# Gates, branch outputs and their gated sum computed with tokens on partitions instead of features on partitions

## The reference, cut to what matters

```python
gates = jax.nn.sigmoid((h @ w_gate + b_gate).astype(jnp.float32)).astype(x.dtype)   # 3 x 1024 columns
g_a, g_b, g_c = jnp.split(gates, N_BRANCH, axis=-1)
merged = g_a * (y_a @ w_br_swa) + g_b * (y_b @ w_br_moba) + g_c * (y_c @ w_br_ssd)
x = x + merged @ w_mix_out
```

## Time and profile before

| | |
|---|---|
| median of 3 runs (lowest, highest) | 1179.04 us (1178.24, 1179.38) |
| profiled execution: its time, its span | 1178.97 us, 1177.2 us |
| PE, PEld busy | 99%, 88% |
| DVE, ACT, POOL busy | 66%, 51%, 5% |
| granted clock of TensorE, mean | 0.999 |
| layer 0: gate a starts / kx starts | 144.02 us / 302.68 us |

### The profile page before, as it was taken

The page is one execution under the profiler, slowest core; times in us unless marked ns, Lnnn a source line. Parts: engine busy times, 40 slices in busy tenths (PEclk is TensorE's granted clock), DMA queues, the critical chain, the costliest instruction groups (busy, mean ns, idle before and its releaser), DMA issues.

```text
span 1177.2 us, 18388 instructions
## 1 busy us (share of the span) xinstructions
PE 1166.1 (99%) x7491; PEld 1036.0 (88%) x7491; DVE 775.1 (66%) x1199; ACT 596.3 (51%) x870; POOL 61.1 (5%) x93
## 2 busy tenths in 40 slices
PE   8999999999999999999999999999999999999997
PEld 7988899999998888888889888999989988888886
DVE  7876856987455475665578677579775455766565
ACT  5656564445454354444455666453555444544443
POOL 1000003300000000000000000033000000000000
PEclk9999999999999999999999999999999999999999
DMA  7744426765644456556456443455755443755660
GB/s 238 237 143 132 156 85 187 220 213 176 194 143 151 136 180 204 188 180 199 159 156 205 144 144 108 140 172 191 250 179 180 144 143 111 244 182 180 202 208 37
DMA packets 156428, 201.31 MB, mean 171 GB/s; under 512 B 7168, under 2 KB 111928, under 8 KB 156344
## 3 DMA queue, kind: packets, MB, share of 16 engines
q1 hardware_dynamic: 155616, 199.58, 53.2%
q10 hardware_dynamic: 728, 0.55, 0.1%
HBM read 199.04 MB, written 1.08 MB: 170 GB/s over the span
## 4 chain that ended last, share of the span: by engine, by line
PE 94%; DMA 2%; DVE 1%; issue 1%; ACT 1%; POOL 1%; SPq 0%; POOLq 0%; DVEq 0%; ACTq 0%
PE psum L1153 12%; PE psum L1154 12%; PE psum L1155 12%; PE psum L1164 11%; PE psum L1165 10%; PE psum L1139 10%; PE psum L1167 10%; PE psum L1140 5%; PE psum L1186 1%; PE psum L1318 1%; PE psum L1356 1%; DMA raw<-in_w_gate_dram 1%; PE psum L1329 1%; PE psum L1374 1%; PE psum L1397 1%
## 5 line engine op out<-in xcount | busy, mean ns | idle before, releaser
L1499 DVE TENSOR_TENSOR w_lo<-raw,w_hi 128x2048 fp32r<-128x2048 f32 (+1 forms) x182 | 408.9, 2251 | 221.3 <-ACT w_hi L755 220.7
L755 ACT ACTIVATE w_hi<-raw 128x2048 fp32r<-128x2048 f32 (+1 forms) x182 | 341.6, 1879 | 158.2 <-PE psum L1167 109.6
L1153 PE MATMUL psum<-act_both,w_hi 128*128 128x256 f32 x832 | 241.0, 290 | 0.0
L1154 PE MATMUL psum<-act_both,w_hi 128*128 128x256 f32 x832 | 235.2, 283 | 0.0
L1155 PE MATMUL psum<-act_both,w_lo 128*128 128x256 f32 x832 | 235.2, 283 | 0.0
L1139 PE MATMUL psum<-act_both,w_hi 128*128 128x512 f32 x512 | 182.1, 400 | 0.0
L1153 PEld LDWEIGHTS psum<-act_both,w_hi 128*128 128x128 f32 x832 | 159.2, 191 | 4.1 <-issue 3.0
L1154 PEld LDWEIGHTS psum<-act_both,w_hi 128*128 128x128 f32 x832 | 159.3, 192 | 0.6 <-issue 0.5
L1155 PEld LDWEIGHTS psum<-act_both,w_lo 128*128 128x128 f32 x832 | 159.2, 191 | 0.0
L1140 PE MATMUL psum<-act_both,w_lo 128*128 128x256 f32 x512 | 143.7, 281 | 0.0
L1139 PEld LDWEIGHTS psum<-act_both,w_hi 128*128 128x128 f32 x512 | 96.2, 188 | 24.6 <-DVE act_both L1528 0.7
(11 more groups left out here) (261 smaller groups left out, 1928.2 us busy)
## 6 DMA issues: line engine op xcount, KB each, us to landing
raw<-in_w_in_dram SPq DMA_DIRECT2D x34, 1024.0 KB, 5.2
raw<-in_w_up_dram SPq DMA_DIRECT2D x32, 1024.0 KB, 5.4
raw<-in_w_down_dram SPq DMA_DIRECT2D x32, 1024.0 KB, 5.0
raw<-in_w_gate_dram SPq DMA_DIRECT2D x24, 1024.0 KB, 7.3
raw<-in_w_ckv_dram SPq DMA_DIRECT2D x16, 1024.0 KB, 5.3
raw<-in_w_br_ssd_dram SPq DMA_DIRECT2D x8, 1024.0 KB, 5.4
raw<-in_w_mix_out_dram SPq DMA_DIRECT2D x8, 1024.0 KB, 5.0
raw<-in_w_cq_dram SPq DMA_DIRECT2D x8, 1024.0 KB, 5.2
```

Of the source, the lines that this page charges most:

```text
L755: act.activation(w_hi[:, slot, 0:n], raw[:, slot, 0:n], ACT.Copy).then_inc(hi_ready.sem, 1)
L1153: pe.matmul(dst, m_hi[:, k, cs], a_hi[:, k, :], start=k == 0, stop=False)
L1154: pe.matmul(dst, m_hi[:, k, cs], a_lo[:, k, :], start=False, stop=False)
L1499: dve.tensor_tensor(w_lo[:, slot, 0:n], raw[:, slot, 0:n], w_hi[:, slot, 0:n].bitcast(F32), ALU.subtract).then_inc(lo_ready.sem, 1)
```

## The change

The gates (12 units a layer), branch_a and branch_b (2 each) and branch_c (4) become units of kind B. `g_sb` and `mg_sb` hold tokens on partitions. The gates' bias now lies along the free dimension, so SP spreads 1024 bias values over all partitions three times a layer (512 KB each), DVE adds them while it reads the bank, and ACT takes the tanh of `g_sb` in place, two pieces of 512 for each pair of gate units. The sum is turned by PE: 8 transposes after unit 39 and 8 between the tiles of unit 41, into two banks each; ACT and DVE split it out of these banks. The turn of the memory's norm moves from slot 41 to slot 42.

```diff
-    stripes_a("gate", "w_gate", 0, "h", 4)
+    stripes_b("gate", "w_gate", 0, "h", 2)
     for j in range(2):
-        unit("branch_a", "A", "w_br_swa", 0, 4, 512 * j, 512, "y_swa", j)
+        stripe_b("branch_a", "w_br_swa", 512 * j, 512, "y_swa", j, (4,))
...
-NORM_TURN_SLOT = {1: U_MIX, 2: U_QX - 2}
+NORM_TURN_SLOT = {1: U_MIX + 1, 2: U_QX - 2}
+MERGED_TURN_SLOT = (U_BRC + 2, U_MIX)
...
+                    for i, (slot, bias) in enumerate(((U_VB, bias_ab), (U_BRB - 1, bias_ab), (U_BRB + 3, bias_c))):
+                        if u == slot:
+                            if i == 1:
+                                sp.wait_ge(*is_read(l, unit_bank(U_BRA - 1, 1)))
+                            if i == 2:
+                                sp.wait_ge(*unit_done.at(l, U_BRA + 2))
+                            sp.dma_start(bias[:], a["b_gate"][l, D * i:D * (i + 1)].partition_broadcast(P))\
+                              .then_inc(bias_loaded.sem, 16)
...
+                if kind == "gate":
+                    for t in range(TT):
+                        g = g_sb[:, t, 512 * j:512 * (j + 1)]
+                        act.wait_ge(*is_read(l, unit_bank(u, t)))
+                        act.activation(g, g, ACT.Tanh, scale=0.5).then_inc(gate_made.sem, 1)
+                    return
...
-                act.wait_ge(*mg_ready.at(l, j + 1))
-                act.activation(act_hi[:, 2 * j:2 * j + 2, :], mg_sb[:, 2 * j:2 * j + 2, :], ACT.Copy, scale=0.5)\
-                   .then_inc(mg_hi.sem, 1)
+                for t in range(TT):
+                    key = ("mergedT", j, t)
+                    act.wait_ge(*is_full(l, key))
+                    act.activation(act_hi[:, 4 * j:4 * j + 4, t * P:(t + 1) * P],
+                                   bank(key).rearrange("p (k n) -> p k n", n=P), ACT.Copy, scale=0.5)\
+                       .then_inc(mg_hi.sem, 1)
...
+                        if t == 1 and u in (U_BRC, U_BRC + 1):
+                            pe.wait_ge(*is_read(l, ("closeT", 6 + u - U_BRC)))
...
+            def merged_turn(l, j):
+
+                for t in range(TT):
+                    key = ("mergedT", j, t)
+                    pe.wait_ge(*mg_ready.at(l, 2 * j + t + 1))
+                    pe.wait_ge(*is_free(l, key))
+                    for k in range(4):
+                        c = 512 * j + k * P
+                        ins = pe.transpose(bank(key)[:, k * P:(k + 1) * P], mg_sb[:, t, c:c + P], ident[:])
+                    ins.then_inc(full(key), 1)
...
+                elif kind == "gate":
+                    branch, cs = w["col"] // D, slice(512 * j, 512 * (j + 1))
+                    dve.wait_ge(*bias_loaded.at(l, 16 * (branch + 1)))
+                    for t in range(TT):
+                        key = unit_bank(u, t)
+                        dve.tensor_tensor(g_sb[:, t, cs], bank(key), (bias_ab, bias_ab, bias_c)[branch][:, cs],
+                                          ALU.add).then_inc(free(key), 1)
...
+                for t in range(TT):
+                    key, ks, ts = ("mergedT", j, t), slice(4 * j, 4 * j + 4), slice(t * P, (t + 1) * P)
+                    dve.wait_ge(*mg_hi.at(l, 2 * j + t + 1))
+                    dve.scalar_tensor_tensor(act_lo[:, ks, ts], bank(key).rearrange("p (k n) -> p k n", n=P), 0.5,
+                                             act_hi[:, ks, ts].bitcast(F32), ALU.mult, ALU.subtract)\
+                       .then_inc(free(key), 1)
```

More of the change, by code:

```diff
@@ L102, in make_units @@
     xbc(5)
[L103 removed]
+    stripes_b("gate", "w_gate", 0, "h", 2)
     for j in range(2):
[L105 to L106 removed]
+        stripe_b("branch_a", "w_br_swa", 512 * j, 512, "y_swa", j, (4,))
+    stripes_b("gate", "w_gate", D, "h", 2)
     for j in range(2):
[L108 to L110 removed]
+        stripe_b("branch_b", "w_br_moba", 512 * j, 512, "y_moba", j, (4,))
+    stripes_b("gate", "w_gate", 2 * D, "h", 2)
+    stripes_b("branch_c", "w_br_ssd", 0, "y_ssd", 2)
     stripes_b("mix", "w_mix_out", 0, "merged", 2)
@@ L248, in slot_banks @@
             out.append((YB_, ("closeT", i)))
+    if s in MERGED_TURN_SLOT:
+        out += [((TB_, OB_)[t], ("mergedT", MERGED_TURN_SLOT.index(s), t)) for t in range(TT)]
     for n in (1, 2):
@@ L840, in evacuate @@
                            .then_inc(z_tanh.sem, 1)
[L841 to L851, removed]
             def relu_high(l, j):
@@ L1015, in _ @@
                         norm_gain_hi(l, 3, ((0, 1), (2, 3))[u - U_CO - 2])
+                    for j in range(2):
+                        if u == MERGED_TURN_SLOT[j] + 1 - j:
+                            merged_hi(l, j)
                     evacuate(l, u)
@@ L1159, in unit @@
                             inner(l, u)
+                        if t == 1 and u in (U_BRC, U_BRC + 1):
+                            pe.wait_ge(*is_read(l, ("closeT", 6 + u - U_BRC)))
+                        if w["act"] == "merged":
+                            part = w["row"] // 512
+                            pe.wait_ge(*mg_hi.at(l, 2 * part + t + 1))
+                            if part == 0:
+                                pe.wait_ge(*is_read(l, ("mergedT", 0, t)))
                         dst = bank(unit_bank(u, t))[:, 0:n]
@@ L1713, in evacuate @@
                     return
-                if not w["last"] or kind in ("qkb", "vb", "kx", "qx", "gate", "down"):
+                if not w["last"] or kind in ("qkb", "vb", "kx", "qx", "down"):
                     return
@@ L1755, in evacuate @@
                                                  ALU.add, ALU.mult).then_inc(free(key), 1)
-                elif kind in ("branch_a", "branch_b", "branch_c"):
-                    for i, key in enumerate(unit_banks(u, w)):
-                        c = w["col"] // P + 2 * i
-                        g, mg = g_sb[:, c:c + 2, :], mg_sb[:, c:c + 2, :]
-                        if i == 0:
-                            wait_read(dve, l, [(v, 0) for v in range(u - 8, u) if UNITS[v]["kind"] == "gate"])
+                elif kind == "gate":
[5 more added lines that the diff above has]
+                                          ALU.add).then_inc(free(key), 1)
+                elif kind in ("branch_a", "branch_b", "branch_c"):
+                    branch = ("branch_a", "branch_b", "branch_c").index(kind)
+                    for t in range(TT):
+                        key, cs = unit_bank(u, t), slice(512 * j, 512 * (j + 1))
+                        g, mg = g_sb[:, t, cs], mg_sb[:, t, cs]
+                        dve.wait_ge(*gate_made.at(l, 4 * branch + 2 * j + t + 1))
+                        if (u, t) == (U_BRC + 3, 1):
+                            dve.wait_ge(*unit_done.at(l, u + 1))
                         if kind == "branch_a":
-                            dve.scalar_tensor_tensor(mg, g, 1.0, two(bank(key)), ALU.add, ALU.mult)\
+                            dve.scalar_tensor_tensor(mg, g, 1.0, bank(key), ALU.add, ALU.mult)\
                                .then_inc(free(key), 1)
                             continue
-                        part = two(tmp[:, i, :])
-                        dve.scalar_tensor_tensor(part, g, 1.0, two(bank(key)), ALU.add, ALU.mult)\
+                        part = tmp[:, t, :]
+                        dve.scalar_tensor_tensor(part, g, 1.0, bank(key), ALU.add, ALU.mult)\
                            .then_inc(free(key), 1)
@@ L1943, in _ @@
                             close_lo_part(l, i)
+                    for j in range(2):
+                        if u == MERGED_TURN_SLOT[j] + 1 - j:
+                            merged_lo(l, j)
                     if 0 <= job_at(u):
@@ L1967, in _ @@
                         norm_gain_lo(l, 3, ((0, 1), (2, 3))[u - U_CO - 2])
-                    if w["kind"] == "branch_c":
-                        merged_lo(l, w["index"])
                     if u == U_CO + 3:
```

50 lines of the change are left out of this document (26 added, 24 removed).

## The result

The changed kernel takes 1198.85 us (median of 4 runs, 1198.25 to 1200.32) against 1179.1 us: a ratio of 1.0172, 95% interval 1.0156 to 1.0187. It is slower by 19.8 us; 1195.5 was forecast. The profiled execution took 1199.17 us, its span 1197.2 us.

A forecast was written before the change was run, and what follows sets the result against it. DVE was taken as full in slots 28 to 34, with PE close behind. Unit 37 7.5 us later plus 0.8 us after it gave 8.3 us a layer, 16.6 us for two: 1195.5 us, 8-in-10 range 1184 to 1203.

The forecast's parts named there:

- The case: Slots 28 to 34: DVE has no spare time, its added work delays PE; unit 37 starts 7.5 us later.
- Where PE waits: PE waits for `y_tok` at the turns of closings 5 and 6, some 2 and 4.5 us, and at unit 37.
- Part 5, the round trip: At a gate stripe's second unit DVE adds, ACT does tanh then `w_hi`, and DVE waits 2.5 us ahead of `w_lo`.
- Part 4, the additions: DVE adds the bias reading two PSUM banks, 0.68 us each, 1.3 us a pair, six pairs a layer.
- Parts 3 and 7, the start of the full stretch: Second bias load costs 0.5 us ahead of unit 30's weights; DVE's stretch without spare time starts 0.6 us earlier, at 201.0.
- The dear price: Rival: the bias load ahead of unit 30 costs 4.6 instead of 0.5 us; 1203.8 us, chance 0.10.
- Part 6, the stall at slot 23: Slot 22's additions and tanh stand ahead of job 15's softmax, so PE stalls 0.6 us.
- Part 1, PE's own gain: PE's matmuls in 20 units a layer gain 0.32 us each, 6.4 us less a layer.
- Part 7's end, from unit 37 on: After unit 37: -1.3 us matmuls, +1.8 us transposes, 0.3 us for the sum's second turn; +0.8 us a layer.
- That DVE and ACT keep up: Rival: PE's own count holds, -4.6 us a layer, 1169.8 us; chance 0.07.
- That the round trip costs nothing: Rival: DVE loses nothing to ACT's `w_hi`, only the additions count; 1.3 us a layer, 1181.6 us; chance 0.08.

The follow-up runs named there:

- experiment 1: Changed kernel with ACT making `w_hi` of unit u + 3 ahead of the two tanh of every gate stripe; 1178.65 us, ratio 1.000 to the kernel before.
- experiment 5: Two kernels: changed kernel with ACT's `w_hi` ahead of the tanh at slots 34 and 36 alone, 1190.19 us; at slots 28 and 30 alone, 1188.38 us.
- experiment 3: Changed kernel with each of DVE's additions of the bias to a bank done twice, same result; 1218.85 us, ratio 1.0336 to the kernel before.
- experiment 4: Changed kernel without the spread of gate b's bias, gate b taking gate a's bias; 1195.61 us, ratio 1.0142 to the kernel before.
- experiment 2: Changed kernel without bias spreads and additions, ACT taking the tanh out of the bank; 1174.9 us, ratio 0.997 to the kernel before.
- experiment 6: Two kernels: changed kernel plus unread PE transposes at slot 31 and ahead of unit 37, 1197.79 us; only the 20 ahead of unit 37, 1195.85 us.

## Why the prediction held, and where it did not

- **The case** was the right one: DVE full in slots 28 to 34, three round trips and three pairs of additions in full, and PE late at unit 37 by what DVE is late. The turn of closing 6 was put at 244.6 and came at 245.43, unit 35 at 249.6 and came at 250.35, unit 37 at 263.6 and came at 264.47. All three are 0.8 to 0.9 us late.
- **Where PE waits** was partly wrong. The forecast had PE come early to the middle of unit 34 and stand there for some 4.5 us for closing 6. It does not stand there: it had lost its lead at the turn of closing 5 (1.73 us), at the start of unit 32 (0.63), in unit 32 at the low clock, and at the start of unit 33 (1.03), where it waits for DVE to read a bank of branch_b. The turn of closing 6 came near its time all the same, because the full DVE sets it either way.
- **Part 5, the round trip,** is shown. Predicted at 2.5 us, measured at 2.50 and 2.51 us in the three places. Experiment 1 takes all of it away, experiment 5 shows it place by place.
- **Part 4, the additions,** 1.3 us a pair, measured 1.28. Their doubling (experiment 3) shows that the three pairs of the full stretch go through.
- **Parts 3 and 7, the start of the full stretch.** The sum put the decays of job 19 at 201.0, so `w_lo` of unit 30 at 198.7. Here is the miss of 0.8 us of layer 0. The load of unit 30, `w_hi` and `w_lo` in the changed kernel:

```profile
189.34 0.43 SPq L659 DMA_DIRECT2D raw<-in_w_gate_dram  x1
...
197.55 1.92 ACT L769 ACTIVATE w_hi<-raw 128x2048 fp32r<-128x2048 f32 x1 [5.35 <-DMA raw<-in_w_gate_dram]
...
199.50 2.29 DVE L1532 TENSOR_TENSOR w_lo<-raw,w_hi 128x2048 fp32r<-128x2048 f32 x1 [3.41 <-ACT w_hi L769]
```

The issue came 0.3 us later than forecast and the landing, 8.2 us after it, 0.4 us later than the 7.3 + 0.5 of the sum. The dear price, 4.6 us, did not come up. What hangs on this row is seen when it is set against unit 37 (us, both counted from the start of unit 20, in the changed kernel 139.49 and 730.84):

| | `w_lo` of unit 30, layers 0 and 1 | unit 37 | between |
|---|---|---|---|
| before | 59.0, 59.9 | 116.7, 117.0 | 57.7, 57.1 |
| changed | 60.0, 58.5 | 125.0, 123.4 | 65.0, 65.0 |
| experiment 4, no second spread | 59.1, 58.0 | 124.3, 123.0 | 65.2, 65.0 |
| experiment 3, additions twice | 64.6, 63.7 | 133.8, 133.0 | 69.3, 69.3 |
| experiment 1, `w_hi` first | 57.9, 57.8 | 116.0, 115.6 | 58.1, 57.8 |

From that row on the forecast has 263.6 - 198.7 = 64.9 us, and 65.0 was measured in both layers: this part of the sum is right to 0.1 us. What varies between layers and kernels is when the row itself comes. In layer 1 it came 1.5 us earlier than in layer 0, which the forecast, the same for both layers, did not have.

- **Part 6, the stall at slot 23,** 0.6 us. It was 1.1: from unit 23 to unit 24 the changed kernel lost 0.9 us against before instead of gaining 0.2. Only a size was off.
- **Part 1, PE's own gain,** 6.4 us a layer, was mis-sized upward: 0.26 and not 0.32 us for a unit that is followed by another kind of work. It could not show in the time, as it was all lost in the waits anyway; in experiment 2, where it counts, it was a part of why I expected too much.
- **Part 7's end, from unit 37 on,** 0.8 us. Measured from unit 37 to kx: 2.4 us in layer 0, 2.65 in layer 1. Here is the miss of the total. About 1.5 of it is unit 37 at the low clock, which stands in no part of the sum. Experiment 6 shows its price by itself: 3.0 us for two layers. The miss is 19.8 - 16.6 = 3.2 us, so this term is nearly all of it. The others cancel, by luck: unit 37 came 0.8 us later than forecast in layer 0, and 1.1 us earlier in layer 1 (6.4 us after before's, counted from unit 20, where 7.5 was said).
- **The rivals.** That DVE and ACT keep up is out for the changed kernel; even with the order of experiment 1 PE still waits for closings (0.51 and 1.43 us in layer 0), and the time is that of the kernel before. That the round trip costs nothing would have been 1181.6 us. Experiment 1, which takes it away, is at 1178.65: the mechanism is sized rightly within 3 us.

Of the clock the rows show that a stretch at 0.50 stands behind a wait of PE: 3.4 us behind the 2.47 us at unit 37. The Trainium skill, page "TensorE: Matmul & The Clock Gate", section "HAM oscillation — how this bites in real kernels", tells the same of groups of matmuls that wait for transfers: the wait sends the clock down and the next group runs slow. The traces agree in kind, with a wait for VectorE in the transfer's place. The waits in the page's example are longer, about 3 to 5 us; here 2.47 us was enough. By the rows of experiment 4, where of two waits of 2.45 us only one brought the fall, the length of the last wait alone does not decide.

## What to carry to other kernels

When an evacuation is split over two engines that also prepare the next operands, look at what stands behind it on the second engine: here one instruction's place on ACT was worth 20 us of 1199; with that order put right, the additions and the bias loads together are worth under 4 (experiments 1 and 2). When one engine is full for a long stretch, look for the load that starts it: a microsecond there came out at the far end in full. When a forecast has TensorE wait for some microseconds, add a term for the clock behind the wait (here about 1.5 us each where nothing later hides it); if the wait can't be removed, filling it can help, at the last wait of a row. Before giving the matrix engine a small matmul, measure its distance to the next one, not its columns.

## What the runs showed of the hardware that I had not expected

- A wait of PE of 2.47 us in the midst of full work was enough to bring the granted clock to 0.50 for 3.4 us. So were waits of 1.73 and 0.63 us shortly after each other (224.23 and 225.52 in layer 0, the fall from 226.5), and in layer 1, with 1.73 us there, it stood at 0.50 for 6.8 us (from 813.6). A wait of 2.45 us did once and once did not (experiment 4); one of 1.04 us did not, but there the clock had fallen 22 us earlier (experiment 5).
- Filling a wait moved the fall to the next one when another engine set the pace (from 226.5 to 234.8 us, from 3.4 to 6.8 us long, in the profiled execution), and removed it at the last wait of the row (experiment 6).
- A matmul with 2 rows of stationary and moving data after ones with 128 costs 0.50 to 0.54 us, against 0.227 us for one of 128 rows and the same 512 columns.
